# A hybrid decoder trunk: a third of the low weight halves made by accumulating transfers instead of GpSimd subtractions

## The chip, the cores and the metric

The kernel runs on one core of one Trainium2 chip. The metric is the device time of one execution in microseconds, given as the median of several runs. The engines are TensorE (PE for its matmuls, PEld for its weight loads), VectorE (DVE), ScalarE (ACT), GpSimd (POOL) and SyncE (SP, which issues most DMA transfers).

## The reference

Two pre-norm residual layers over 256 tokens of width 1024, all in float32. Each layer projects the normalised tokens by one matrix, feeds four token mixers with the parts, gates, projects and merges their outputs, and projects once more:

```
h = rms_norm(x, norm_g)
proj = einsum('bsd,de->bse', h, w_in)
u_lru, u_s5, qkv_ret, q_nsa, kv_nsa, bg_nsa, gate_paths, merge = split_columns(proj, IN_SIZES)
...                                    # four mixers: y_lru, y_s5, y_ret, y_nsa, each (256, 512)
ys = stack([y_lru, y_s5, y_ret, y_nsa]) * silu(gate_paths)
branch = einsum('bsnw,nwd->bsnd', ys, w_branch)
merged = sum(sigmoid(merge) * branch, axis=n)
x = x + einsum('bsd,de->bse', merged, w_out)
```

A final RMSNorm closes the stack. The inputs of both layers amount to over 100 MB of weights, each used once per execution.

## The kernel before

The products with the large weight matrices are cut into 36 chunks per layer (`CHUNKS`, lines 42 to 51), each a block of up to 512 output columns, and 34 of these into units (`UNITS`) of two 128-row slabs of 512 columns: 128 x 1024 numbers, 512 KB. There are 108 units a layer. SP loads them in order into a ring of four buffers, `raw` (`load_unit`, line 412; the loop at line 581). Transfers are issued in order, and each waits until its buffer is free.

The first 48 units of a layer are multiplied as they are ("native", lines 1515 to 1524). The last 60, `SPLIT_UNITS`, are split: a weight w becomes a high half, w rounded to the type `fp32r`, and a low half, w minus the high half; the activations are split in the same way. Each product is then three matmuls (`split_product`, line 1477): high x high, high x low, low x high. A split unit takes 12 matmuls of 512 columns on TensorE (24 of 256 columns in the two `glu` chunks). In this text the split units of a layer are numbered 0 to 59. Units 0 to 3 belong to the GLU of the S5 mixer, 4 to 7 to the gate of the retention branch, 8 to 11 to the first branch projection, 12 to 19 to a merge gate, and so on; 56 to 59 are the last of the output projection.

A split unit goes through these steps:

- SP loads it into `raw`.
- ScalarE casts it into `w_hi` (`cast_units`, line 664; the activation is recorded at line 660) and counts `hi_done`.
- GpSimd subtracts `w_hi` from `raw` into `w_lo` (`split_lo`, lines 632 to 643) and counts `lo_done`. For units 56 to 59 VectorE does that and counts `vlo_done`.
- TensorE waits for the low half (`wait_low`, line 377), which implies the high one.
- SP may load into the same `raw` buffer again when the low half is done (line 603).

`w_hi` and `w_lo` are rings of five (`N_SPLIT`): ScalarE and GpSimd wait for TensorE to be done with the unit five places earlier. Every engine runs its instructions in the order in which they are written. On ScalarE the casts stand between the other activations of the mixers: the casts of units 0 to 4 ahead of the eight gate activations of the RG-LRU mixer, those of 5 to 7 behind them, 8 to 11 behind the split of the first gated mixer output (`hi_of_gated`), 12 to 15 behind a square root and a table load, and in the sparse attention at the end some between the exponentials of one group of heads and the next (`attention_exp`, `cast_room`). On TensorE the chunks stand between the small products of the mixers. The compressed attention scores pass through a chain of small operations on VectorE (lines 1340 to 1357) whose result TensorE transposes ahead of the attention scores of the first group of heads.

Of the kernel before, what the change touches and what calls it, by code (L numbers as in the profile page):

```python
# [16 lines left out]
P = 128  # L17
# [3 lines left out]
DEPTH = 2  # L21
# [40 lines left out]
NU = len(UNITS)  # L62
for _u in range(NU):
    UNIT_USED.append((UNIT_USED[-1] if _u else 0) + (_u + 1 != UNIT_END[UNITS[_u][0]]))
N_RAW = 4
# [1 line left out]


NATIVE = ("u_s5", "cmp", "u_lru", "ret_v", "nsa_kv", "gate_s5", "gate_lru", "merge_s5_0", "merge_s5_1", "ret_q", "ret_k", "nsa_q")
SPLIT_UNITS = [u for u in range(NU) if CHUNKS[UNITS[u][0]][0] not in NATIVE]  # L70


LO_ON_VECTOR = ("out_0b", "out_1b")
VECTOR_UNITS = [u for u in SPLIT_UNITS if CHUNKS[UNITS[u][0]][0] in LO_ON_VECTOR]


def slot(s, l):
# [9 lines left out]
def vector_splits(upto):  # L87

    return sum(u < upto for u in VECTOR_UNITS)

V_NORM, V_CONV, V_CONVB, V_BA, V_BX, V_LAM, V_D, V_BGLU, V_LR, V_LI, V_DT, V_ROWS = (
# [7 lines left out]
    "cw1_loaded": 128, "cw_done": 1, "cw_loaded": 32, "diag_done": 2, "dt_exp": 1, "dt_rows": 1, "evacuated0": 16,  # L102
    "evacuated1": 16, "gate_tanh": 2, "h_done": 8, "hfull_done": 8, "hhi_done": 4, "hi_done": 60, "hidT_done": 2,
    "hid_arg": 1, "hid_ready": 1, "hid_tanh": 1, "hid_tm_ready": 2, "hlo_done": 8, "kcT_done": 1, "kcT_ready": 1,
    "kc_ready": 1, "lam_abs": 1, "lam_exp": 1, "lo_done": 56, "lru_act": 16, "lru_m2": 1, "lru_mm": 1,
    "lru_sqrt": 1, "mT_done": 2, "mag_arg": 1, "mag_exp": 1, "mhi_done": 2, "mlo_done": 2, "mt_free": 6,
    "nT_done": 2, "nT_ready": 2, "noT_done": 1, "no_cmp": 1, "nrope_ready": 2, "out_token": 2, "qkT_done": 2,
    "qkT_ready": 2, "raw_loaded0": 448, "raw_loaded1": 448, "raw_loaded2": 448, "raw_loaded3": 448, "rnT_done": 1,
    "rn_ready": 1, "ro_done": 4, "rope_ready": 2, "rrstd": 1, "rs_done": 4, "rs_ready": 4, "rstd": 2, "rvar": 1,
    "s5_split": 2, "sq": 4, "th_ready": 1, "th_sin": 3, "trig_done": 24, "unit_used": 73, "var": 2, "vbd_ready": 1,  # L110
    "vecT": 2, "vec_ready": 1, "vectors_loaded": 208, "vlo_done": 4, "wl_loaded": 64, "xT_done": 4, "x_half": 3,
    "xc_ready": 1, "y_done": 8, "y_used": 4, "yg_hi": 4, "yg_lo": 4, "yg_ready": 4, "yr_ready": 1, "z_arg": 1,
    "z_hi": 1, "z_lo": 1, "z_ready": 1, "z_tanh": 1}

TWO_PI = 2.0 * math.pi
PI2_A = 6.28125
# [57 lines left out]
def hybrid_trunk(nc, a, out):  # L174
# [4 lines left out]
    with ctx:  # L179
# [125 lines left out]
        raw_loaded = [sem(f"raw_loaded{i}") for i in range(N_RAW)]  # L305
        hi_done, lo_done, vlo_done, unit_used = sem("hi_done"), sem("lo_done"), sem("vlo_done"), sem("unit_used")
        chunk_done = sem("chunk_done")
        evacuated = [sem("evacuated0"), sem("evacuated1")]
        dve_order = sem("dve_order")
        xT_done = sem("xT_done")  # L310
# [66 lines left out]
        def wait_low(eng, u):  # L377


            if u in VECTOR_UNITS:  # L380
                eng.wait_ge(vlo_done, vector_splits(u + 1))
            else:
                eng.wait_ge(lo_done, splits(u + 1) - vector_splits(u + 1))

        def pr(name):

# [22 lines left out]
            return ap.to_broadcast(shape)  # L409


        def load_unit(sp, u, l, signal):

            c, k, n, w = UNITS[u]
            name = CHUNKS[c][0]
            dst = raw[:, u % N_RAW, 0:n * w].rearrange("p (k n) -> p k n", k=n)

            def load(d, src):
                sp.dma_start(d, src.rearrange("(k p) n -> p k n", p=P)).then_inc(signal, 16)

            def w_in(col, width, d=None):
                load(dst if d is None else d, a["w_in"][l][k * P:(k + n) * P, col:col + width])

            kind = name.split("_")[0]
            half = 512 * int(name[4] if kind == "out" else name[-1]) if kind in ("merge", "branch", "out") else 0
            if kind == "u":
                w_in(COL_S5 if name == "u_s5" else COL_LRU, w)
            elif kind == "ret":
                w_in(COL_RET + BW * "qkv".index(name[-1]), w)
            elif name == "nsa_q":  # L430
                w_in(COL_NQ, w)
            elif name == "nsa_kv":
# [107 lines left out]
        with nc.Block() as block:  # L540
            for l in range(DEPTH):
                @block.sync
                def _(queue):
# [37 lines left out]
                    for u in range(N_RAW, NU):  # L581
# [14 lines left out]
                        if u == UNIT_END[CHUNK["merge_nsa_0"]]:  # L596
# [2 lines left out]
                                load_vectors(queue, l + 1, VECTORS_A + VECTORS_B)  # L599
                            else:  # L600
                                queue.dma_start(g_row, a["final_norm_g"].unsqueeze(0).to_broadcast([P, D])).then_inc(g_loaded, 16)
                        if u - N_RAW in SPLIT_UNITS:
                            wait_low(sp, u - N_RAW)
                        else:
                            wait_unit_read(sp, u - N_RAW)
# [10 lines left out]
                def _(pool):  # L616
# [13 lines left out]
                    def split_lo(upto):  # L630

                        for s in range(done[0], splits(upto)):
                            u = SPLIT_UNITS[s]
                            c, _, n, w = UNITS[u]
                            if u in VECTOR_UNITS:
                                continue
                            gp.wait_ge(hi_done, s + 1)
                            if s >= N_SPLIT:
                                wait_unit_read(gp, SPLIT_UNITS[s - N_SPLIT])
                            elif l:  # L640
                                Layer(pool, l - 1).wait_ge(x_half, 3)
# [13 lines left out]
                def _(scalar):  # L655
# [8 lines left out]
                    def cast_units(upto):  # L664

                        for s in range(done[0], splits(upto)):
# [5 lines left out]
                            elif l:  # L672
                                Layer(scalar, l - 1).wait_ge(x_half, 3)
                            run(w_hi[:, slot(s, l), 0:n * w], raw[:, u % N_RAW, 0:n * w], ACT.Copy, hi_done)
                        done[0] = max(done[0], splits(upto))

                    def next_cast(name):
# [792 lines left out]
                def _(tensor):  # L1470
# [12 lines left out]
                    def chunk(name, part=2):  # L1483
# [11 lines left out]
                        for n in todo:  # L1495
                            u = u0 + n
                            _, k0, nk, _ = UNITS[u]
                            if name in NATIVE:
                                pe.wait_ge(raw_loaded[u % N_RAW], raw_target[u])
                            else:  # L1500
                                wait_low(pe, u)
# [1 line left out]
                            for kk in range(nk):  # L1503
# [8 lines left out]
                                def ht(lo, hi, pair=(h_hi, h_lo)):  # L1512
                                    return tuple(t[:, k, lo:hi] for t in pair)

                                if name in NATIVE:
                                    rw = raw[:, u % N_RAW, kk * w:(kk + 1) * w]
                                    if name in ("u_s5", "u_lru", "gate_s5", "gate_lru"):
                                        for m in range(4):
# [2 lines left out]
                                    else:  # L1521
                                        for t in range(TT):
                                            last = mm(ps[:, 512 * t:512 * t + w], h_full[:, k, t * P:(t + 1) * P], rw,  # L1523
                                                      start=st_, stop=sp_, skip_group_check=True)
                                elif kind == "u":
                                    for m in range(4):
                                        last = split_product(ps[:, m * T:(m + 1) * T], wt(m * P, (m + 1) * P), ht(0, T), st_ and m % 2 == 0, sp_)
                                elif kind == "glu":
# [361 lines left out]
```

## Time and profile before

| | |
|---|---|
| median of 3 runs | 858.96 us (858.77 to 859.5) |
| the profiled execution's own time | 857.93 us |
| its span in the trace | 856.1 us |
| PE busy | 825.7 us (96%) |
| DVE busy | 561.5 us (66%) |
| ACT busy | 312.2 us (36%) |
| POOL busy | 294.9 us (34%) |
| DMA, mean | 148 GB/s, 126.56 MB |

The two layers follow each other, and the second half of each has the split units: in the trace these lie at about 205 to 430 us and 626 to 850 us. GpSimd has next to nothing to do outside these stretches. A busy share tells little by itself here: what counts is whether a half is ready when TensorE comes to it. A timeline row gives the start and the length of an instruction, or of several alike that follow each other without a pause (then with their count behind the x).

### The profile page before, as it was taken

What the parts mean: (1) busy time and instruction counts of PE and PEld (TensorE: products, weight loads), DVE (VectorE), ACT (ScalarE), POOL (GpSimd) and SP (SyncE); (2) the same over time, 40 slices, a digit from 0 to 9 for tenths busy, and PEclk for the clock granted to TensorE, in tenths of its full rate; (3) what the DMA queues carried; (4) which work ended last, traced back from release to release, by engine and by line L of the source; (5) the groups of instructions that cost most, each with busy time, mean ns of one, the idle gap of its engine ahead of it and who ended that gap; (6) DMA issues with size and microseconds to landing.
All of it is one profiled execution on the core that took longest, in us unless ns stands there. A gap on an engine that the chain in (4) does not pass through costs nothing.

```text
span 856.1 us, 10220 instructions
## 1 busy us (share of the span) xinstructions
PE 825.7 (96%) x3918; PEld 611.4 (71%) x3918; DVE 561.5 (66%) x939; ACT 312.2 (36%) x519; POOL 294.9 (34%) x130
## 2 busy tenths in 40 slices
PE   8999999999899799999999999999998989999996
PEld 8864774446778688888888558644486867888885
DVE  2978999483697652634657889993828974435335
ACT  4411211015743545454425112110173534554542
POOL 1000000005567576767000000000157676665760
PEclk9999999999999899999999999999999998999999
DMA  8575544445245444444535745444554344445541
GB/s 250 140 245 144 192 127 122 130 141 201 94 127 168 123 148 148 120 152 152 153 70 161 244 119 198 143 125 127 146 172 147 116 132 129 137 130 170 172 147 50
DMA packets 86992, 126.56 MB, mean 148 GB/s; under 512 B 22072, under 2 KB 32672, under 8 KB 86944
## 3 DMA queue, kind: packets, MB, share of 16 engines
q1 hardware_dynamic: 86768, 125.88, 48.4%
q8 instruction: 31, 0.51, 0.2%
q14 instruction: 17, 0.14, 0.0%
q10 hardware_dynamic: 176, 0.04, 0.0%
HBM read 124.85 MB, written 1.05 MB: 147 GB/s over the span
## 4 chain that ended last, share of the span: by engine, by line
PE 59%; issue 29%; POOL 5%; DVE 3%; DMA 1%; ACT 1%; ACTq 0%; SPq 0%; POOLq 0%; DVEq 0%
PE proj L1480 29%; PE proj L1523 12%; PE proj L1519 6%; POOL w_lo L642 5%; PE M L1475 3%; PE M L1783 1%; PE M L1788 1%; DVE sc L1357 1%; PE M L1480 1%; DMA mt<-in_nsa_cv_w 1%; PE M L1753 1%; PE M L1807 1%; PE M L1806 1%; PE M L1624 1%; PE M L1805 1%
## 5 line engine op out<-in xcount | busy, mean ns | idle before, releaser
L642 POOL TENSOR_TENSOR w_lo<-raw,w_hi 128x1024 fp32r<-128x1024 f32 x112 | 286.3, 2586 | 504.9 <-ACT w_hi L660 473.9
L1523 PE MATMUL proj<-raw,h_full 128*128 128x512 f32 (+1 forms) x512 | 213.2, 572 | 0.0
L1523 PEld LDWEIGHTS proj<-raw,h_full 128*128 128x128 f32 x512 | 95.5, 190 | 104.7 <-issue 100.7
L660 ACT ACTIVATE w_hi<-raw 128x1024 fp32r<-128x1024 f32 x120 | 122.6, 1050 | 65.8 <-PE proj L1480 27.3
L1480 PE MATMUL proj<-w_hi,h_hi 128*128 128x512 f32 x320 | 128.4, 401 | 0.9 <-POOL w_lo L642 0.9
L1480 PE MATMUL proj<-w_lo,h_hi 128*128 128x512 f32 x320 | 124.9, 390 | 0.0
L1480 PE MATMUL proj<-w_hi,h_lo 128*128 128x512 f32 x320 | 124.8, 390 | 0.0
L1519 PE MATMUL proj<-h_full,raw 128*128 128x256 f32 x512 | 113.8, 381 | 0.0
L1519 PEld LDWEIGHTS proj<-h_full,raw 128*128 128x128 f32 x512 | 96.2, 190 | 14.1 <-issue 0.8
L1480 PEld LDWEIGHTS proj<-w_hi,h_hi 128*128 128x128 f32 x320 | 60.1, 188 | 14.4 <-issue 1.7
L1480 PEld LDWEIGHTS proj<-w_hi,h_lo 128*128 128x128 f32 x320 | 60.1, 188 | 13.0
L1480 PEld LDWEIGHTS proj<-w_lo,h_hi 128*128 128x128 f32 x320 | 60.2, 188 | 12.0 <-issue 0.5
L1480 PE MATMUL proj<-w_hi,ys_hi 128*128 128x512 f32 x128 | 52.9, 413 | 5.2 <-POOL w_lo L642 5.1
L1480 PE MATMUL proj<-w_lo,ys_hi 128*128 128x512 f32 x128 | 52.0, 406 | 0.0
L1480 PE MATMUL proj<-w_hi,ys_lo 128*128 128x512 f32 x128 | 51.9, 405 | 0.0
L660 ACT ACTIVATE sc<-sc,st 128x256 f32<-128x256 f32 x64 | 28.2, 442 | 57.2 <-DVE st L1373 57.2
L1123 DVE SCALAR_TENSOR_TENSOR mt<-mt,proj 128x1024 f32<-128x1024 f32 x12 | 14.7, 1222 | 39.6 <-PE proj L1480 39.6
L660 ACT ACTIVATE mt<-proj 128x1024 f32<-128x1024 f32 x16 | 16.3, 1019 | 63.1 <-PE proj L1523 54.4
L660 ACT ACTIVATE sc<-sc 128x512 f32<-128x512 f32 (+2 forms) x38 | 23.5, 665 | 42.0 <-DVE sc L1214 37.4
L1480 PEld LDWEIGHTS proj<-w_hi,ys_hi 128*128 128x128 f32 x128 | 25.4, 198 | 12.0 <-issue 5.9
L1480 PEld LDWEIGHTS proj<-w_hi,ys_lo 128*128 128x128 f32 x128 | 25.2, 197 | 5.6
L1480 PEld LDWEIGHTS proj<-w_lo,ys_hi 128*128 128x128 f32 x128 | 25.2, 197 | 5.2
(293 smaller groups left out, 1208.6 us busy)
## 6 DMA issues: line engine op xcount, KB each, us to landing
raw<-in_w_in SPq DMA_DIRECT2D x152, 512.0 KB, 3.5
raw<-in_w_branch SPq DMA_DIRECT2D x32, 512.0 KB, 3.8
raw<-in_w_out SPq DMA_DIRECT2D x16, 512.0 KB, 3.7
raw<-in_s_w_glu SPq DMA_DIRECT2D x8, 512.0 KB, 3.7
raw<-in_w_in SPq DMA_DIRECT2D x8, 256.0 KB, 2.6
merged<-in_nsa_ck_w SPq DMA_DIRECT2D x4, 512.0 KB, 5.3
mt<-in_nsa_ck_w SPq DMA_DIRECT2D x4, 512.0 KB, 6.9
merged<-in_nsa_cv_w SPq DMA_DIRECT2D x4, 512.0 KB, 5.8
```

Source lines behind the costliest of these rows:

```text
L642: nc.gpsimd.tensor_tensor(w_lo[:, slot(s, l), 0:n * w], raw[:, u % N_RAW, 0:n * w], w_hi[:, slot(s, l), 0:n * w].bitcast(f32), ALU.subtrac ...
L660: i = nc.scalar.activation(out_, in_, func, **kw)
L1123: v.scalar_tensor_tensor(m, m, 1.0, src, ALU.add, ALU.mult).then_inc(evac(full), 1)
L1357: i = v.tensor_tensor(cp[:, e_], cmp_s[:, e_], bc(coef[:, e_].unsqueeze(3), shape), ALU.mult)
L1475: return nc.tensor.transpose(dst, src, ident[0:rows_, 0:rows_])
L1480: last = mm(dst, left[i], right[j], start=start and n == 0, stop=stop and n == 2, skip_group_check=True)
L1519: last = mm(ps[:, m * T:(m + 1) * T], rw[:, m * P:(m + 1) * P], h_full[:, k, :], start=st_ and m % 2 == 0, stop=sp_, skip_group_check=True)
L1523: last = mm(ps[:, 512 * t:512 * t + w], h_full[:, k, t * P:(t + 1) * P], rw, start=st_, stop=sp_, skip_group_check=True)
L1624: last = mm(dst, cT[:, f, q, r], s5_h[:, p % 2, f, j, :], start=f == 0, stop=f == 1)
L1753: last = mm(M[:, e, at:at + 16], nqT[r, h, t * P:(t + 1) * P], kcT[r, (h // 2) * 16:(h // 2) * 16 + 16], start=True, stop=True)
L1783: last_ = mm(M[:, 2, at:at + P], nqT[r, 2 * h + n, 0:P], nkT[r, i, 0:P], start=True, stop=True)
L1788: mm(M[:, e, n * T:(n + 1) * T], nqT[r, 2 * h + n, P:T], nkT[r, i, :], start=True, stop=True)
```

## The change

Of the 56 split units whose low half GpSimd makes, every third (1, 4, 7, ..., 55; 19 a layer) gets it in another way. ScalarE, right after its cast, also writes the negated high half into `w_lo` (an activation Copy with scale -1, counted by `neg_done`). GpSimd waits for that and issues a DMA transfer that reads the unit's weights a second time from HBM and adds them onto `w_lo` (`accum_op=ALU.add`). TensorE waits for the landing of that transfer, on a semaphore of the `w_lo` buffer (`lo_added`). SP may refill the `raw` buffer of such a unit when the cast is done. `load_unit` takes the destination and the accumulate option as new arguments. The tests that told native chunks by name now ask whether the unit is split; the same units as before are native.

```diff
+ADDED_UNITS = [u for n, u in enumerate(v for v in SPLIT_UNITS if v not in VECTOR_UNITS) if n % 3 == 1]
...
+def added_splits(upto):
+
+    return sum(u < upto for u in ADDED_UNITS)
+
+
+def added_count(u, l):
+
+    here = slot(splits(u), l)
+    return sum((m, w) <= (l, u) and slot(splits(w), m) == here for m in range(DEPTH) for w in ADDED_UNITS)
...
             if u in VECTOR_UNITS:
                 eng.wait_ge(vlo_done, vector_splits(u + 1))
+            elif u in ADDED_UNITS:
+                eng.engine.wait_ge(lo_added[slot(splits(u), eng.l)], 16 * added_count(u, eng.l))
             else:
-                eng.wait_ge(lo_done, splits(u + 1) - vector_splits(u + 1))
+                eng.wait_ge(lo_done, splits(u + 1) - vector_splits(u + 1) - added_splits(u + 1))
...
-        def load_unit(sp, u, l, signal):
+        def load_unit(sp, u, l, signal, into=None, **how):
...
-            dst = raw[:, u % N_RAW, 0:n * w].rearrange("p (k n) -> p k n", k=n)
+            dst = (raw[:, u % N_RAW, 0:n * w] if into is None else into).rearrange("p (k n) -> p k n", k=n)
 
             def load(d, src):
-                sp.dma_start(d, src.rearrange("(k p) n -> p k n", p=P)).then_inc(signal, 16)
+                sp.dma_start(d, src.rearrange("(k p) n -> p k n", p=P), **how).then_inc(signal, 16)
...
-                        if u - N_RAW in SPLIT_UNITS:
+                        if u - N_RAW in ADDED_UNITS:
+                            sp.wait_ge(hi_done, splits(u - N_RAW + 1))
+                        elif u - N_RAW in SPLIT_UNITS:
                             wait_low(sp, u - N_RAW)
...
+                            if u in ADDED_UNITS:
+                                gp.wait_ge(neg_done, added_splits(u + 1))
+                                load_unit(pool, u, l, lo_added[slot(s, l)], w_lo[:, slot(s, l), 0:n * w], accum_op=ALU.add)
+                                continue
                             gp.wait_ge(hi_done, s + 1)
...
                             run(w_hi[:, slot(s, l), 0:n * w], raw[:, u % N_RAW, 0:n * w], ACT.Copy, hi_done)
+                            if u in ADDED_UNITS:
+                                act.wait_ge(hi_done, s + 1)
+                                run(w_lo[:, slot(s, l), 0:n * w], w_hi[:, slot(s, l), 0:n * w].bitcast(f32), ACT.Copy, neg_done, scale=-1.0)
```

On GpSimd, the first low halves of layer 0 stood in a row as follows (`w_lo<-raw,w_hi` is the subtraction; the first row has units 0 to 4):

```order
L642 TENSOR_TENSOR w_lo<-raw,w_hi 128x1024 [waits hi_done] x5
L642 TENSOR_TENSOR w_lo<-raw,w_hi 128x1024 [waits unit_used,hi_done]
L642 TENSOR_TENSOR w_lo<-raw,w_hi 128x1024 [waits chunk_done,hi_done]
L642 TENSOR_TENSOR w_lo<-raw,w_hi 128x1024 [waits unit_used,hi_done]
L642 TENSOR_TENSOR w_lo<-raw,w_hi 128x1024 [waits chunk_done,hi_done]
```

With the change GpSimd's row for units 0 to 8 is this (line numbers are those of the changed file):

```order
L671 TENSOR_TENSOR w_lo<-raw,w_hi 128x1024 [waits hi_done]
L442 DMA w_lo<-in_s5_w_glu 128x2x512 [waits neg_done]
L671 TENSOR_TENSOR w_lo<-raw,w_hi 128x1024 [waits hi_done] x2
L442 DMA w_lo<-in_w_in 128x2x512 [waits neg_done]
L671 TENSOR_TENSOR w_lo<-raw,w_hi 128x1024 [waits unit_used,hi_done]
L671 TENSOR_TENSOR w_lo<-raw,w_hi 128x1024 [waits chunk_done,hi_done]
L442 DMA w_lo<-in_w_in 128x2x512 [waits neg_done]
L671 TENSOR_TENSOR w_lo<-raw,w_hi 128x1024 [waits chunk_done,hi_done]
```

The transfer of a unit stands where its subtraction stood, and waits for ScalarE's negation instead of its cast.

On ScalarE, units 3 to 5 stood as follows around the gate activations of the RG-LRU mixer (`sc<-M,small` and `sc<-sc,small`):

```order
L660 ACTIVATE w_hi<-raw 128x1024 [waits raw_loaded3]
L660 ACTIVATE u_s<-proj 128x1024 [waits chunk_done]
L660 ACTIVATE w_hi<-raw 128x1024 [waits raw_loaded0]
L660 ACTIVATE sc<-M,small 128x256 [waits lru_mm]
L660 ACTIVATE sc<-M,small 128x256 x7
L847 ACT_TABLE_LOAD
L660 ACTIVATE sc<-sc,small 128x256 [waits lru_act]
L660 ACTIVATE sc<-sc,small 128x256 x7
L660 ACTIVATE w_hi<-raw 128x1024 [waits unit_used,raw_loaded1]
```

With the change the same place on ScalarE reads:

```order
L689 ACTIVATE w_hi<-raw 128x1024 [waits raw_loaded3]
L689 ACTIVATE u_s<-proj 128x1024 [waits chunk_done]
L689 ACTIVATE w_hi<-raw 128x1024 [waits raw_loaded0]
L689 ACTIVATE w_lo<-w_hi 128x1024 [waits hi_done]
L689 ACTIVATE sc<-M,small 128x256 [waits lru_mm]
L689 ACTIVATE sc<-M,small 128x256 x7
L879 ACT_TABLE_LOAD
L689 ACTIVATE sc<-sc,small 128x256 [waits lru_act]
L689 ACTIVATE sc<-sc,small 128x256 x7
L689 ACTIVATE w_hi<-raw 128x1024 [waits unit_used,raw_loaded1]
```

The negation of unit 4 now stands ahead of the gate activations, and the cast of unit 5 still behind them. TensorE's row is the same as before.

## Rows read from the trace of the kernel before

**Rows 1.** The page's busy us, shares and instructions of each engine.
```profile
PE 825.7 (96%) x3918; PEld 611.4 (71%) x3918; DVE 561.5 (66%) x939; ACT 312.2 (36%) x519; POOL 294.9 (34%) x130
```

**Rows 2.** Waits of PE: who for whom, us in total, times, longest us.
```profile
PE M L1475 <- DVE sc L1357: 9.1, 2, 4.5
PE proj L1480 <- POOL w_lo L642: 6.0, 4, 2.6
```

**Rows 3.** The page's costliest groups: busy us, mean ns, idle before and releaser.
```profile
L642 POOL TENSOR_TENSOR w_lo<-raw,w_hi 128x1024 fp32r<-128x1024 f32 x112 | 286.3, 2586 | 504.9 <-ACT w_hi L660 473.9
L660 ACT ACTIVATE w_hi<-raw 128x1024 fp32r<-128x1024 f32 x120 | 122.6, 1050 | 65.8 <-PE proj L1480 27.3
```

**Rows 4.** Timeline, 282 to 287.5 us: start, us, engine, line, operation, [idle before].
```profile
282.15 4.73 DVE L1357 TENSOR_TENSOR sc<-sc,st 128x128 f32<-128x128 f32 x2
...
284.34 2.39 POOL L642 TENSOR_TENSOR w_lo<-raw,w_hi 128x1024 fp32r<-128x1024 f32 x1
...
286.94 0.67 PE L1475 MATMUL M<-const,sc 128*128 128x128 f32 x2 [4.54 <-DVE sc L1357]
```

**Rows 5.** Windows: us, busy (x) PE, PEld, DVE, ACT, POOL; PEclk, DMA share, GB/s.
```profile
235.80:239.20 3.40, 3.40 (x10) 2.63 (x9) 3.40 (x2) 0.02 (x1) 3.40 (x2) 0.50 0.77 217
287.00:293.80 6.80, 6.80 (x24) 5.57 (x25) 2.25 (x3) 1.33 (x2) 4.39 (x2) 0.50 0.76 223
```

**Rows 6.** Timeline of PE: the first product of unit 8.
```profile
234.74 0.47 PE L1480 MATMUL proj<-w_hi,ys_hi 128*128 128x512 f32 x1 [2.56 <-POOL w_lo L642]
```

**Rows 7.** DMA issues: count, KB each, median us from issue to landing.
```profile
raw<-in_w_branch SPq DMA_DIRECT2D x32, 512.0 KB, 3.8
...
mt<-in_nsa_ck_w SPq DMA_DIRECT2D x4, 512.0 KB, 6.9
```

**Rows 8.** The chain that ended last: start us, us, what.
```profile
430.59 0.55 POOL st L522
```

**Rows 9.** Timeline of ACT: casts of units 4, then 8 to 11.
```profile
208.15 1.05 ACT L660 ACTIVATE w_hi<-raw 128x1024 fp32r<-128x1024 f32 x1
209.09 3.02 ACT L660 ACTIVATE sc<-M,small 128x256 f32<-128x256 f32 x8
...
231.03 3.88 ACT L660 ACTIVATE w_hi<-raw 128x1024 fp32r<-128x1024 f32 x4
```

**Rows 10.** Timelines of DVE, POOL and PE around unit 7.
```profile
227.19 1.58 DVE L1272 SCALAR_TENSOR_TENSOR sc<-sc 128x1024 f32<-128x1024 f32 x1 [1.77 <-ACT sc L660]
...
224.30 3.38 POOL L642 TENSOR_TENSOR w_lo<-raw,w_hi 128x1024 fp32r<-128x1024 f32 x1
...
227.98 0.39 PE L1480 MATMUL proj<-w_hi,h_hi 128*128 128x512 f32 x1
```

**Rows 11.** Timelines of POOL and PE: subtraction and first product of unit 13.
```profile
252.31 2.77 POOL L642 TENSOR_TENSOR w_lo<-raw,w_hi 128x1024 fp32r<-128x1024 f32 x1
...
255.32 0.39 PE L1480 MATMUL proj<-w_hi,h_hi 128*128 128x512 f32 x1
```

**Rows 12.** Timeline of ACT: casts of units 25, 31, 37 and 43.
```profile
298.75 1.04 ACT L660 ACTIVATE w_hi<-raw 128x1024 fp32r<-128x1024 f32 x1
...
322.53 1.04 ACT L660 ACTIVATE w_hi<-raw 128x1024 fp32r<-128x1024 f32 x1
...
345.18 1.04 ACT L660 ACTIVATE w_hi<-raw 128x1024 fp32r<-128x1024 f32 x1
...
369.06 1.04 ACT L660 ACTIVATE w_hi<-raw 128x1024 fp32r<-128x1024 f32 x1
```

**Rows 13.** The chain: units 24 and 25, 30 and 31, 36 and 37, 42 and 43.
```profile
305.05 5.48 PE proj L1480 x24
...
327.67 5.51 PE proj L1480 x24
...
350.31 5.51 PE proj L1480 x24
...
372.96 5.51 PE proj L1480 x24
```

More of the change, by code:

```diff
@@ L69, with by_name @@
 NATIVE = ("u_s5", "cmp", "u_lru", "ret_v", "nsa_kv", "gate_s5", "gate_lru", "merge_s5_0", "merge_s5_1", "ret_q", "ret_k", "nsa_q")
-SPLIT_UNITS = [u for u in range(NU) if CHUNKS[UNITS[u][0]][0] not in NATIVE]
+def by_name(u):
+    return CHUNKS[UNITS[u][0]][0]
+SPLIT_UNITS = [u for u in range(NU) if by_name(u) not in NATIVE]
 LO_ON_VECTOR = ("out_0b", "out_1b")
-VECTOR_UNITS = [u for u in SPLIT_UNITS if CHUNKS[UNITS[u][0]][0] in LO_ON_VECTOR]
+VECTOR_UNITS = [u for u in SPLIT_UNITS if by_name(u) in LO_ON_VECTOR]
+ADDED_UNITS = [u for n, u in enumerate(v for v in SPLIT_UNITS if v not in VECTOR_UNITS) if n % 3 == 1]
 def slot(s, l):
@@ L104 @@
     "hid_arg": 1, "hid_ready": 1, "hid_tanh": 1, "hid_tm_ready": 2, "hlo_done": 8, "kcT_done": 1, "kcT_ready": 1,
-    "kc_ready": 1, "lam_abs": 1, "lam_exp": 1, "lo_done": 56, "lru_act": 16, "lru_m2": 1, "lru_mm": 1,
+    "kc_ready": 1, "lam_abs": 1, "lam_exp": 1, "lo_done": 37, "lru_act": 16, "lru_m2": 1, "lru_mm": 1,
     "lru_sqrt": 1, "mT_done": 2, "mag_arg": 1, "mag_exp": 1, "mhi_done": 2, "mlo_done": 2, "mt_free": 6,
[L107 to L113, printed above, removed]
+    "nT_done": 2, "nT_ready": 2, "neg_done": 19, "noT_done": 1, "no_cmp": 1, "nrope_ready": 2, "out_token": 2,
+    "qkT_done": 2, "qkT_ready": 2, "raw_loaded0": 448, "raw_loaded1": 448, "raw_loaded2": 448, "raw_loaded3": 448,
+    "rnT_done": 1, "rn_ready": 1, "ro_done": 4, "rope_ready": 2, "rrstd": 1, "rs_done": 4, "rs_ready": 4,
+    "rstd": 2, "rvar": 1, "s5_split": 2, "sq": 4, "th_ready": 1, "th_sin": 3, "trig_done": 24, "unit_used": 73,
+    "var": 2, "vbd_ready": 1, "vecT": 2, "vec_ready": 1, "vectors_loaded": 208, "vlo_done": 4, "wl_loaded": 64,
+    "xT_done": 4, "x_half": 3, "xc_ready": 1, "y_done": 8, "y_used": 4, "yg_hi": 4, "yg_lo": 4, "yg_ready": 4,
+    "yr_ready": 1, "z_arg": 1, "z_hi": 1, "z_lo": 1, "z_ready": 1, "z_tanh": 1}
 TWO_PI = 2.0 * math.pi
@@ L307, in hybrid_trunk @@
         chunk_done = sem("chunk_done")
+        neg_done = sem("neg_done")
+        lo_added = [sem(f"lo_added{i}") for i in range(N_SPLIT)]
         evacuated = [sem("evacuated0"), sem("evacuated1")]
@@ L1497, in chunk @@
                             _, k0, nk, _ = UNITS[u]
-                            if name in NATIVE:
+                            if u not in SPLIT_UNITS:
                                 pe.wait_ge(raw_loaded[u % N_RAW], raw_target[u])
@@ L1513, in ht @@
                                     return tuple(t[:, k, lo:hi] for t in pair)
-                                if name in NATIVE:
+                                if u not in SPLIT_UNITS:
                                     rw = raw[:, u % N_RAW, kk * w:(kk + 1) * w]
@@ L1524, in chunk @@
                                                       start=st_, stop=sp_, skip_group_check=True)
-                                elif kind == "u":
+                                elif name in ("u_s5", "u_lru", "gate_s5", "gate_lru"):
                                     for m in range(4):
```

## The prediction

> **What bounds the kernel now.** I read the busy shares first, then TensorE's waits, then the margins in the second half of a layer (the only part that is changed), and last the durations from which the new step is priced. TensorE is busy 825.7 of 856.1 us [rows 1], so there are some 30 us to win in all. Of its waits the trace names two that reach the weights' low halves: 9.1 us in 2 waits for VectorE's line 1357, one in each layer, and 6.0 us in 4 waits for GpSimd's subtraction [rows 2]. GpSimd is therefore no bound over the span; it matters where TensorE stands right behind it. I number the 60 split units of a layer 0 to 59, in the order of use; the change takes 1, 4, 7 and so on up to 55 (19 of them). All times below are of layer 0; layer 1 repeats the pattern 420.6 us later, as the two equal waits of rows 2 say.
>
> **What is removed.** 38 subtractions of 2.59 us each on GpSimd [rows 3], 98 us of its work, and with each of them its hold on an input that VectorE shares: in the trace two VectorE operations on 128x128 elements, an elementwise product each, take 4.73 us together while GpSimd subtracts, and the subtraction of unit 22 fills exactly the second half of that stretch, 284.34 to 286.73 [rows 4]. TensorE stands still for 4.54 us for that result, to 286.94 [rows 4]. Without that subtraction the second product can start at 284.4 as the first ends: 2.3 us less wait in each layer. TensorE is granted half speed, the lower of 1.2 and 2.4 GHz, from 287.0 to 293.8 after that standstill, and from 235.8 to 239.2 after the shorter one of 2.56 us [rows 5, 6]. At half speed half of the time is lost: 3.4 us of the longer stretch, 1.7 us of the shorter. The shorter wait should bring the shorter slow stretch: 1.7 us more. The gain is 2.3 + 1.7 = 4.0 us a layer. The Trainium skill (SBUF — State Buffer, Who interferes with whom) says that a VectorE instruction with two SBUF inputs is shut out for the whole of a GpSimd instruction that reads SBUF; the trace agrees with it in the 4.73 us, and the new transfer's descriptors are no such instruction.
>
> **What is added.** ScalarE gets 38 negations of the size of its casts, 1.05 us each [rows 3], with a wait for its own cast ahead, about 0.05 us. Then GpSimd issues, and the transfer lands. Call D the time from the moment at which both the negation and GpSimd's work ahead are over to the landing. The trace of before has no DMA from GpSimd and none that adds, so D is bounded from its neighbours. Low: 3.5 us, no dearer than a plain 512 KB load (3.8 us at the median [rows 7]) with the issue free and a little luck. High: 9.5 us, if GpSimd is held as long as by a subtraction (2.6 [rows 3]) and the landing is as slow as that of the slower group of 512 KB loads, several in flight (6.9 [rows 7]). I take 0.6 for the issue (a tiny GpSimd operation takes 0.55 [rows 8]), 3.8 for a plain load, and half of that again, 1.9, because the destination must be read as well: D = 6.3, close to the 6.9 of rows 7. The raw loads go on beside it, on the same engines, and the weights of these units are read twice, 38 x 512 KB = 19.9 MB more.
>
> The Trainium skill (DMA: Bandwidth & Descriptors, Anatomy of one DMA — SWDGE (gpsimd) path) gives a transfer from GpSimd a fixed 2.0 us and its bytes at 436 GB/s; counted for both operands, 1.05 MB, that is an estimate of 4.4 us. No row of this trace shows such a transfer.
>
> **Place by place, for D = 6.3.** A unit is late if cast end + 1.1 (or the end of GpSimd's work ahead, if later) + D passes the moment TensorE wants it.
> - Unit 8, and 4 and 7 ahead of it. The negation of unit 4 stands between its cast at 208.15 and the gate activations at 209.09 [rows 9]. VectorE and then the cast of unit 8 at 231.03 hang on these, and TensorE waits for unit 8 until 234.74 [rows 6, 9]. So +1.1, less 0.4 because VectorE's line 1272 (1.58 us, behind unit 7's subtraction [rows 10]) gets free: 235.4. Unit 7 itself: GpSimd is free for it at 224.30 [rows 10] + 1.1 = 225.4, lands 231.7, wanted at 227.98 [rows 10] + 1.1; 2.6 late. From unit 7's start to unit 8's are 4.2 us of TensorE work (231.7 + 4.2 = 235.9): net +1.2.
> - Unit 13. GpSimd reaches it at 252.31, TensorE wants it at 255.32, and now it is ready just in time [rows 11]. Landing at 252.35 + 6.3 = 258.65: +3.3. A standstill of that size brought half speed before, so +1.7.
> - Units 31, 37 and 43 have casts at 322.53, 345.18 and 369.06 [rows 12]; each is the second half of a run of 24 products that starts at 327.67, 350.31 and 372.96 [rows 13], so wanted 2.6 later: 330.3, 352.9, 375.6. Cast end + 1.1 + 6.3 is 331.0, 353.6, 377.5: +0.7, +0.7, +1.9.
> - Unit 25: its cast ends at 299.8 and it is wanted 2.6 us into the run from 305.05, at 307.6 [rows 12, 13]; 299.8 + 7.4 = 307.2, so nothing, with 0.4 to spare. The same difference of cast end and use is 7 us or more for the other 12 (1, 10, 16, 19, 22, 28, 34, 40, 46, 49, 52, 55), and GpSimd has no queue ahead of them that uses it up: nothing. The 1.05 us of the negations there lie in ScalarE's gaps. If that cover were gone, each negation would cost its 1.1 us, as at unit 4. Nothing is queued on GpSimd behind a wait for a negation that TensorE needs at once: the next cast comes 1.05 us later, where a subtraction of 2.4 is saved.
> - SP gets the raw slot back at the cast instead of the subtraction, 1.3 us or more earlier. Raw data is not what TensorE waits for, so it gives nothing and only brings loads beside the new transfers.
>
> Sum: 1.2 + 3.3 + 1.7 + 0.7 + 0.7 + 1.9 - 4.0 = 5.5 us a layer, 11.0 in all. On the profiled execution's own 857.93 us that is 868.9; the median of the runs is 1.0 above that execution, so 869.9: **870 us**.
>
> **The rivals.**
> 1. *A short transfer, and the change is faster.* For D = 3.5: unit 8 +0.7, unit 13 +0.5 (255.85 against 255.32), the rest in time, gain 4.0: -2.8 a layer, -5.6 in all, 853 us. For D = 4.4: unit 13 +1.4, unit 8 +0.7, so -1.9 a layer: 855 us. For it: the plain load's 3.8 us at the median, and that only the landing of the last byte counts. Against it: the issue and the second operand would have to be nearly free. The skill's estimate of 4.4 us above falls here. Chance 0.28.
> 2. *No difference.* At D = 4.7 to 4.9 unit 13's 1.8 and its possible half speed, unit 8's 0.7 and unit 43's 0.3 meet the 4.0. 859 us. Chance 0.10.
> 3. *A slow transfer.* For D = 7.7: unit 8 +2.6, unit 13 +4.7 and 2.5 of half speed, unit 25 +1.0 (299.8 + 1.1 + 7.7 against 307.6), units 31, 37, 43 +2.1, +2.1, +3.3 with 3.4 of half speed, less 4.0: 17.7 a layer, 894 us. At D = 9.5 it passes 910. For it: two raw loads are set free just when unit 13's transfer is issued, and share the engines. Chance 0.15.
> 4. *The relief of VectorE does not come*, because writing the descriptors shuts VectorE out as the subtraction did: then the 4.0 a layer is not gained, 878 us. The trace can't exclude it: it shows only subtractions beside VectorE. Chance 0.05.
>
> The forecast itself has 0.42; its own range, D from 5.5 to 7, is 861 to 883.
>
> **How the numbers follow.** From about D = 4.7 on the change costs. The range goes from D = 3.5 to a little over 7.7: 852 to 896, leaving out the slowest part of rival 3. A measurement can tell about 0.2% (1.7 us) from nothing. Slower: forecast, rivals 3 and 4, 0.62. Same: 0.10. Faster: 0.28.
>
> **What will show it.** Right, if the page of the changed kernel has a transfer into w_lo from GpSimd with 5.5 to 7 us from issue to landing; if TensorE's waits have a new row that ends with that DMA, longest 2 to 4 us, at unit 13; if the wait for line 1357 falls from 9.1 to about 4.5 us; and if ScalarE has 38 more operations of 1.05 us. Wrong, if that landing takes under 4.7 us, or if the late units are others: then it is an engine's queue, and not the transfer, that decides. If the wait for line 1357 stays at 9.1, rival 4 holds.

## The result, and the profile after

The changed kernel takes 897.24 us at the median of four runs (895.58 to 898.63), against 858.87 us for the kernel before on the same chip: a ratio of 1.0449, with a 95% interval of 1.0426 to 1.0472. The profiled execution took 895.58 us, its span is 893.8 us and its mean granted TensorE clock 0.967, against 0.987 before. The forecast said slower, by 11 us; it is slower by 38 us, just above the range.

From the page of the changed kernel, against [rows 1, 3, 7]: the busy line, the two groups of GpSimd and the new one of ScalarE (busy us, mean ns | idle before, with what ended it), and two issue rows (KB each, median us from issue to landing). Line 671 is the subtraction (642 before), line 442 the new transfer, line 689 the activations of ScalarE (660 before), line 1512 the split products (1480 before), line 1389 the old 1357, and line 1157 the old 1125, the sum of the merge. (In the experiments' kernels the same lines stand one or two further down, or, where nothing is transferred, a few further up.)

```profile
PE 838.1 (94%) x3918; PEld 620.3 (69%) x3918; DVE 561.4 (63%) x939; ACT 351.5 (39%) x557; POOL 233.5 (26%) x130
...
L671 POOL TENSOR_TENSOR w_lo<-raw,w_hi 128x1024 fp32r<-128x1024 f32 x74 | 188.0, 2617 | 459.5 <-ACT w_hi L689 449.6
...
L442 POOL DMA_DIRECT2D w_lo<-in_w_in x24 | 29.0, 1206 | 98.9 <-ACT w_lo L689 98.4
...
L689 ACT ACTIVATE w_lo<-w_hi 128x1024 fp32r<-128x1024 f32 x38 | 40.3, 1060 | 1.2
...
w_lo<-in_w_in POOLq DMA_DIRECT2D x24, 512.0 KB, 6.9
...
w_lo<-in_w_branch POOLq DMA_DIRECT2D x8, 512.0 KB, 8.8
```

What was to be moved has moved: 38 subtractions are gone, 38 negations of 1.06 us are there, and 38 x 512 KB come a second time. GpSimd is less busy by 61 us and TensorE more busy by 12.4 us for the same 3918 products, which I read as time at the lower clock. The span grew by 37.7 us, so the other 25.3 us are standstills. Which ones, the waits of TensorE say (us in total, times, longest):

```profile
PE proj L1512 <- DMA w_lo<-in_w_in: 14.6, 9, 5.3
PE M L1507 <- DVE sc L1389: 11.5, 2, 5.7
PE proj L1512 <- DMA w_lo<-in_s_w_glu: 4.9, 2, 3.5
PE M L1507 <- DVE merged L1157: 4.7, 2, 2.4
PE proj L1512 <- DMA w_lo<-in_w_branch: 3.5, 2, 2.8
```

Against [rows 2]: the 6.0 us for GpSimd's subtractions are gone, 23.0 us in 13 waits for the new transfers have come, the wait behind VectorE's product has grown from 9.1 to 11.5 us where it was to be halved, and there is a new one at line 1157.

Laying the two timelines of TensorE side by side, unit by unit, gives what each place cost in both layers together, the slow clock behind it included (a unit's lateness against before, less that of the unit ahead):

| place | forecast, both layers | measured in the two traces |
|---|---|---|
| unit 1, with the wait for ScalarE behind it | 0 | +8.9 |
| units 7 to 9 | +2.4 | -0.5 (layer 0 -3.6, layer 1 +3.1) |
| unit 10 | 0 | +3.5 |
| units 12 and 13 | +10.0 | +9.8 (unit 12 -1.3, unit 13 +11.0) |
| VectorE's line 1389, ahead of unit 20 | -8.0 | +3.2 |
| units 31, 37, 43 | +6.6 | +3.2 |
| line 1157, ahead of unit 51 | 0 | +8.2 |
| elsewhere | 0 | +1.3 |
| sum | +11.0 | +37.6 |

The measured column compares one execution of each kernel, and a single place in it is good to a few us only. Layer 0 up to unit 13 is the same program in two of the kernels below (the one without unit 52's transfer, and the changed kernel with a wait), yet units 12 and 13 cost 5.8 and 8.9 us there, and here 2.3. Here the granted clock stayed at 1.00 behind the standstill of 2.63 us; without unit 52's transfer it was 0.50, half speed, behind one of 3.05 us.

In layer 1, 2.1 us of what stands under unit 1 are a wait for ScalarE: 2.88 us instead of 0.81 for the gate activations of the RG-LRU mixer, ahead of which unit 4's cast waited 0.97 us for its raw load and the negation took 1.06.

Three things stand behind the table. The first is how long the transfer takes. Of the 38, eleven land 5.6 to 5.9 us after the issue, six after 6.4 to 6.7, and the other 21 after 7.0 to 10.5. GpSimd and SP around the transfer of unit 13, then GpSimd around that of unit 31 (start us, us, what; in brackets the idle time before and what ended it):

```profile
252.86 1.20 POOL L442 DMA_DIRECT2D w_lo<-in_w_in  x1
253.64 5.16 POOL L671 TENSOR_TENSOR w_lo<-raw,w_hi 128x1024 fp32r<-128x1024 f32 x2
...
252.94 6.26 SPq L442 DMA_DIRECT2D raw<-in_w_in  x4
...
262.35 0.50 PE L1512 MATMUL proj<-w_hi,h_hi 128*128 128x512 f32 x1 [2.63 <-DMA w_lo<-in_w_in]
...
333.58 1.20 POOL L442 DMA_DIRECT2D w_lo<-in_w_in  x1 [9.37 <-ACT w_lo L689]
...
339.32 0.50 PE L1512 MATMUL proj<-w_hi,h_hi 128*128 128x512 f32 x1 [0.35 <-DMA w_lo<-in_w_in]
```

At unit 31 SP's next load goes out only 4 us later (the one before it went out 1.46 us ahead of the transfer): the first packet moves 1.9 us after the issue, and TensorE goes on 5.74 us after it. At unit 13 SP issues two raw loads 0.1 and 0.5 us after GpSimd: the first packet moves only after 4.9 us, and TensorE goes on after 9.49. From 1.0 to 4.5 us behind the issue only packets of the raw loads move. That is no chance meeting. SP issues in order. The subtraction of unit 12 sets unit 12's raw slot free, unit 13's has been free since its cast, and the end of that same subtraction is what lets GpSimd go on to its transfer. So wherever GpSimd has no gap between a subtraction and the next transfer, two raw loads start beside it.

The second is VectorE's product. VectorE and GpSimd at the place of [rows 4]:

```profile
289.31 5.92 DVE L1389 TENSOR_TENSOR sc<-sc,st 128x128 f32<-128x128 f32 x2
...
286.83 4.73 POOL L671 TENSOR_TENSOR w_lo<-raw,w_hi 128x1024 fp32r<-128x1024 f32 x2 [9.87 <-PE proj L1512]
291.49 1.22 POOL L442 DMA_DIRECT2D w_lo<-in_w_branch  x1
292.26 2.81 POOL L671 TENSOR_TENSOR w_lo<-raw,w_hi 128x1024 fp32r<-128x1024 f32 x1
...
295.29 0.69 PE L1507 MATMUL M<-const,sc 128*128 128x128 f32 x2 [5.74 <-DVE sc L1389]
```

The subtraction of unit 22 is gone, but that of unit 23 takes its place 0.77 us after the issue began, and takes 2.81 us instead of 2.39: so the two products take 5.92 us instead of 4.73, where 2.4 was forecast. The clock shows the price of the longer standstill (us, busy times, then the granted clock; before it was 6.8 us at half speed [rows 5], here 6.8 us, to 302.2, behind a stretch with almost no product in it):

```profile
292.00:295.40 3.40, 0.11 (x1) 0.11 (x2) 3.23 (x1) 0.00 (x0) 3.07 (x2) 0.55 0.82 225
295.40:298.80 3.40, 3.40 (x15) 2.88 (x15) 0.00 (x0) 1.33 (x2) 1.38 (x1) 0.50 1.07 224
```

The third was nowhere in the forecast: an elementwise sum of VectorE, 1024 wide, now coincides with a subtraction behind the transfer of unit 52.

```profile
411.52 3.72 DVE L1157 TENSOR_TENSOR merged<-merged,mt 128x1024 f32<-128x1024 f32 x1
...
408.20 1.20 POOL L442 DMA_DIRECT2D w_lo<-in_w_out  x1 [1.93 <-ACT w_lo L689]
408.97 5.18 POOL L671 TENSOR_TENSOR w_lo<-raw,w_hi 128x1024 fp32r<-128x1024 f32 x2
...
415.30 1.97 PE L1507 MATMUL M<-const,merged 128*128 128x128 f32 x8 [2.35 <-DVE merged L1157]
```

### The profile page after: what moved, and what is told of

Same layout as the page of the kernel before. It is cut to its first block, busy times and chain, and to the rows that moved or that the text cites. A ratio compares the mean times of both kernels' runs of the same rounds, so it can differ in the third digit from the quotient of the medians.

```text
span 893.8 us, 10222 instructions
## 1 busy us (share of the span) xinstructions
PE 838.1 (94%) x3918; PEld 620.3 (69%) x3918; DVE 561.4 (63%) x939; ACT 351.5 (39%) x557; POOL 233.5 (26%) x130
## 4 chain that ended last, share of the span: by engine, by line
PE 58%; issue 14%; POOL 9%; DMA 8%; DVE 8%; ACT 2%; SPq 0%; ACTq 0%; POOLq 0%; DVEq 0%
PE proj L1555 23%; PE proj L1512 15%; PE proj L1551 10%; POOL w_lo L671 7%; DMA w_lo<-in_w_in 6%; PE M L1507 2%; PE M L1512 2%; DVE sc L1389 1%; PE M L1656 1%; DMA raw<-in_s_w_glu 1%; PE M L557 1%; POOL w_lo L442 1%; ACT w_hi L689 1%; DMA mt<-in_nsa_cv_w 1%; PE M L1785 1%
## 5 line engine op out<-in xcount | busy, mean ns | idle before, releaser
L671 POOL TENSOR_TENSOR w_lo<-raw,w_hi 128x1024 fp32r<-128x1024 f32 x74 | 188.0, 2617 | 459.5 <-ACT w_hi L689 449.6
L1512 PE MATMUL proj<-w_hi,h_hi 128*128 128x512 f32 x320 | 131.6, 411 | 14.8 <-DMA w_lo<-in_w_in 14.6
L1512 PE MATMUL proj<-w_lo,h_hi 128*128 128x512 f32 x320 | 127.0, 397 | 0.0
L1512 PE MATMUL proj<-w_hi,h_lo 128*128 128x512 f32 x320 | 126.6, 395 | 0.0
L442 POOL DMA_DIRECT2D w_lo<-in_w_in x24 | 29.0, 1206 | 98.9 <-ACT w_lo L689 98.4
L689 ACT ACTIVATE w_lo<-w_hi 128x1024 fp32r<-128x1024 f32 x38 | 40.3, 1060 | 1.2
```

What stands on the lines that cost most here:

```text
L442: sp.dma_start(d, src.rearrange("(k p) n -> p k n", p=P), **how).then_inc(signal, 16)
L689: i = nc.scalar.activation(out_, in_, func, **kw)
L1512: last = mm(dst, left[i], right[j], start=start and n == 0, stop=stop and n == 2, skip_group_check=True)
```

## The experiments

Each ratio is against runs of the kernel before on the same chip, whose medians were 858.4, 858.5 and 857.0 us in the three groups. The lists of units are set by one line; where a variant transfers other units, the counts per layer follow it.

**Is it the adding?** The transfer without its addition, all else as changed.

```
-  load_unit(pool, u, l, lo_added[slot(s, l)], w_lo[:, slot(s, l), 0:n * w], accum_op=ALU.add)
+  load_unit(pool, u, l, lo_added[slot(s, l)], w_lo[:, slot(s, l), 0:n * w])
```

> The changed kernel with plain transfers instead of accumulating ones (the low halves are then the full weights, so the output is not the reference's). Theory Q (queueing: in the trace of the changed kernel a transfer that is issued together with two raw loads sends its first packet 4 to 5 us later and lands after 7.7 to 10 us, one alone after 5.6 to 5.9): the slow ones stay slow, median landing 6.5 us or more, 887 to 897 us. Theory A (the adding itself, a read and a write of the destination, makes the transfer long): landing falls to that of a raw load, 3.5 to 5 us, everywhere, and the time to 865 to 875 us.

877.07 us, 1.0219 [1.0198, 1.0240]. Issue row, and the two waits that answer to it:

```profile
w_lo<-in_w_in POOLq DMA_DIRECT2D x24, 512.0 KB, 5.1
```

```profile
PE M L1507 <- DVE sc L1389: 10.6, 2, 5.3
PE proj L1512 <- DMA w_lo<-in_w_in: 7.7, 4, 3.6
```

A plain transfer lands 4.3 to 5.2 us after its issue when alone, 4.7 in the middle (first packet after 1.6 us), and 5.0 to 7.5 beside two raw loads (after some 2.9), and its issue is a row of 0.74 us on GpSimd instead of 1.20. So the addition costs 1 us alone and about 3 us beside raw loads, and with it go 20 of the 38 us. The other half stays with a transfer that adds nothing: VectorE's wait and the queueing (the first packet that comes late beside raw loads) are there too. Neither theory has the whole.

**Is it the raw loads beside it?** SP holds the first of the two raw loads, and with it those behind it, until the transfer has landed.

```
+  if u - N_RAW + 1 in ADDED_UNITS:
+      wait_low(sp, u - N_RAW + 1)
```

> SP holds back the raw load that was issued at the same moment as each accumulating transfer, until that transfer has landed. Theory Q: every landing takes 5.5 to 6.6 us, TensorE's waits for w_lo transfers fall from 23 us to below 10, and the time to 872 to 886 us, unless raw data becomes late. Theory A and theory V (VectorE or the next subtraction holds back the writing of descriptors): landings stay at 7.7 to 10 us in the same places, time 893 us or more.

942.05 us, 1.0976 [1.0949, 1.1003]. Its issue row, then the wait for the transfers:

```profile
w_lo<-in_w_in POOLq DMA_DIRECT2D x24, 512.0 KB, 5.9
```

```profile
PE proj L1514 <- DMA w_lo<-in_w_in: 18.4, 12, 4.0
```

The landing falls from 6.9 to 5.9 and from 8.8 to 6.5 us at the median, over all 38 from 7.4 to 6.0 (5.7 to 8.1). The subtraction behind the issue still starts 0.78 us after it at most places, and the first packet moves after 1.9 us there: the raw loads beside the transfer delay it, not that subtraction. The time is not won, because SP issues in order: the held load holds those behind it, casts come late (ScalarE waits 73.6 us for raw loads of `in_w_in`, 1.0 us in the changed kernel), and with them the transfers. TensorE's waits for them add up to 37 us, where below 10 was expected, and the time is 56 us above the upper end of what was expected; holding loads back is no cure.

**One unit where the overlap is certain.** Only unit 13 is transferred.

```
-  ... if n % 3 == 1]
+  ... if n == 13]
```

> Only unit 13 of each layer comes by transfer. Two raw loads are set free with its issue. Theory Q (queueing behind them): it lands about 9 us after the issue, 6 us after TensorE wants it, with a slow-clock stretch behind: 8 to 10 us a layer, 874 to 880 us. If the landing were the 5.7 us of an undisturbed transfer: 3.3 us late, 5 us a layer, 868 to 870 us. The price of the prediction for this unit was 5.0 us a layer.

875.60 us, 1.0199 [1.0167, 1.0232]. Its waits:

```profile
PE proj L1513 <- DMA w_lo<-in_w_in: 12.8, 2, 7.1
PE M L1508 <- DVE sc L1390: 9.1, 2, 4.5
PE proj L1513 <- POOL w_lo L672: 6.0, 4, 2.6
```

The two transfers land 10.25 and 8.85 us after the issue, with two raw loads issued 0.1 and 0.5 us behind each. TensorE waits 7.1 and 5.7 us for them and has half speed for a while after; everything else is as before. That is 9 us a layer for one unit, where the forecast's sum had 5.0. In the changed kernel unit 13 costs 11.0 us in both layers together: in the first TensorE comes to it 4 us late already, where GpSimd is only 0.6 us late, and stands 2.6 us without a slow clock behind it; in the second it stands 5.3 us, with half speed behind.

**Only the units with much time to spare**, 16, 19, 22, 28, 34, 40, 46, 49, 52 and 55.

```
-  ... if n % 3 == 1]
+  ... if n in (16, 19, 22, 28, 34, 40, 46, 49, 52, 55)]
```

> Only 10 units a layer come by transfer, those whose cast ended 7.5 us or more before use (16, 19, 22, 28, 34, 40, 46, 49, 52, 55). If only late landings at 1, 7, 10, 13, 31, 37, 43 cost: no TensorE wait on a transfer, 858 to 866 us, the rest being VectorE waits of changed phase. If each transfer or negation costs for itself, 10 of 19: about 879 us.

884.16 us, 1.0299 [1.0271, 1.0328]: far from expected. Waits, then GpSimd around the issue of unit 16:

```profile
PE M L1508 <- DVE sc L1390: 11.4, 2, 5.7
PE proj L1513 <- DMA w_lo<-in_w_in: 9.8, 2, 4.9
```

```profile
260.72 3.36 POOL L672 TENSOR_TENSOR w_lo<-raw,w_hi 128x1024 fp32r<-128x1024 f32 x1
264.02 1.34 POOL L443 DMA_DIRECT2D w_lo<-in_w_in  x1
...
266.59 5.13 POOL L672 TENSOR_TENSOR w_lo<-raw,w_hi 128x1024 fp32r<-128x1024 f32 x2
```

Unit 16 is cast at 259.56, but GpSimd still has subtractions to do and issues at 264.02; the transfer lands 9.25 us later, and TensorE stands 4.90 us, until 273.41. The time from cast to use was not to spare: with units 7, 10 and 13 subtracted again, GpSimd's queue used it up. The waits for VectorE are those of the changed kernel.

**The late units only**, from 25 on (11 a layer).

```
-  ... if n % 3 == 1]
+  ... if n % 3 == 1 and n >= 25]
```

> Only units 25 to 55 (11 a layer) by transfer, none in the first part. From the trace of the changed kernel: units 31, 37 and 43 some 1.5 us a layer together, unit 51 about 4 us: 867 to 872 us. It would be 880 us or more if transfers cost in proportion to their number (11 of 19 of the loss).

870.92 us, 1.0154 [1.0124, 1.0184]. Its waits:

```profile
PE M L1508 <- DVE merged L1158: 4.8, 2, 2.4
PE proj L1513 <- DMA w_lo<-in_w_in: 3.5, 6, 0.8
```

As expected: some 14 us, of which the late units' own waits are 3.5 us, in six waits (31, 37 and 43 of each layer), and the sum of line 1157 (1158 here) 4.8. With what the clock adds the two places cost 5.4 and 5.1 us. That leaves some 24 us of the loss for units 1 to 22.

**VectorE and what stands behind the issue.** First unit 22 alone, then 22 and 23, so that no subtraction follows the issue at once.

```
-  ... if n % 3 == 1]
+  ... if n == 22]            # the other kernel: n in (22, 23)
```

> Only unit 22 of each layer comes by transfer; all else as before. Theory P (the prediction: without the subtraction of unit 22 VectorE's second product starts as the first ends): the TensorE wait for line 1389 (1357 before) falls from 9.1 to about 4.5 us, 850 to 853 us. Theory S (as the trace of the changed kernel suggests, the issue and the subtraction of unit 23 behind it shut VectorE out in its place): the wait is 9 to 12 us, 859 to 865 us. The trace tells what VectorE's second product waits out.

> Units 22 and 23 of each layer come by transfer, so no subtraction stands behind unit 22 on GpSimd until unit 24. Theory S (a subtraction behind the issue shuts VectorE out): the wait for line 1389 falls to about 4.5 us, 850 to 855 us. Theory V (the issue itself, the writing of descriptors, shuts VectorE out): the second product ends with the first issue, 1.2 us later than under S, or with the second; the wait is 6 to 8 us or more.

Unit 22 alone: 861.63 us, 1.0041 [1.0028, 1.0054]. VectorE and GpSimd:

```profile
281.82 6.07 DVE L1390 TENSOR_TENSOR sc<-sc,st 128x128 f32<-128x128 f32 x2
...
284.00 1.35 POOL L443 DMA_DIRECT2D w_lo<-in_w_branch  x1
284.94 2.80 POOL L672 TENSOR_TENSOR w_lo<-raw,w_hi 128x1024 fp32r<-128x1024 f32 x1
```

Units 22 and 23: 854.21 us, 0.9957 [0.9944, 0.9970], faster than before. The same view, then TensorE's waits:

```profile
281.82 2.60 DVE L1390 TENSOR_TENSOR sc<-sc,st 128x128 f32<-128x128 f32 x2
...
284.00 2.59 POOL L443 DMA_DIRECT2D w_lo<-in_w_branch  x2
286.48 2.54 POOL L672 TENSOR_TENSOR w_lo<-raw,w_hi 128x1024 fp32r<-128x1024 f32 x1
...
PE M L1508 <- DVE sc L1390: 4.8, 2, 2.4
PE proj L1513 <- DMA w_lo<-in_w_branch: 4.5, 4, 1.3
```

The issue of a transfer does not shut VectorE out: the first product ends with the subtraction ahead, at 284.1, and the second runs while the two transfers are issued, so that both are done at 284.42. One more subtraction 0.94 us behind the issue does, for its whole length. So the relief is real and can be had, but not by taking unit 22 alone. By place it brings 5.3 and 4.9 us in the two layers, slow clock included (the forecast had 4.0), and 2.8 us of it in each go to the two transfers, of which the second lands 13.0 us after its issue.

**ScalarE's share.** The negations stay, every unit is subtracted, no transfer is issued.

```
-  load_unit(pool, u, l, lo_added[slot(s, l)], w_lo[...], accum_op=ALU.add)
-  continue
```

> The negations stay on ScalarE, in w_lo, but GpSimd subtracts all 56 low halves as before and there are no added transfers. If ScalarE's 38 x 1.06 us matter only at unit 4 (and so unit 8): +1.1 us a layer, perhaps a changed phase beside it, 859 to 864 us. If ScalarE's work is what costs: 880 us or more.

864.29 us, 1.0073 [1.0046, 1.0100]: about 6 us, somewhat more than expected. Its waits:

```profile
PE M L1501 <- ACT sc L683: 3.7, 2, 1.9
...
PE M L1501 <- DVE u_s L1277: 2.5, 2, 2.1
```

The forecast charged one negation of 1.1 us a layer. ScalarE's work is late at several places by about a negation each. VectorE's sum of line 1157 (1151 here) is waited for 0.9 us in each layer already, with no transfer in the kernel.

**Line 1157.** The changed kernel without the transfer of unit 52.

```
-  ... if n % 3 == 1]
+  ... if n % 3 == 1 and n != 52]
```

> The changed kernel without the transfer of unit 52. In its trace VectorE's line 1157 is shut out by the subtraction behind that issue, and TensorE loses 2.35 us and a slow-clock stretch at unit 51, about 4 us a layer. If that subtraction's changed start is the cause: the wait goes, 8 us less, 887 to 890 us. If it is chance of the whole schedule: unchanged, 895 us or more.

891.02 us, 1.0380 [1.0351, 1.0408]: 6.2 us less than the changed kernel by the medians, 5.9 by the ratios, a little short of expected. The wait for line 1157 is gone from TensorE's waits. In the changed kernel the transfer of unit 52 lands in time; what it costs is that the next subtraction meets VectorE's sum.

**GpSimd made to wait for VectorE's chain.** One wait ahead of unit 20's subtraction, so that nothing of GpSimd runs beside lines 1340 to 1357: in the kernel before (first), and in the changed one (second).

```
+  if s == 20:
+      gp.wait_ge(cp_ready, 1)
```

> The kernel before, with no transfer on GpSimd; GpSimd waits for the end of VectorE's chain up to line 1357 before it subtracts unit 20, whose low half was ready 9.3 us before use. If the three subtractions of units 20 to 22 are what lengthens that chain from about 2 to 6.7 us, TensorE's 4.5 us wait goes, and the slow-clock stretch of 6.8 us behind it, up to 8 us a layer: 843 to 850 us. If VectorE was slow for itself: no change or slower.

> The changed kernel with the wait of b1_cp on GpSimd ahead of unit 20. If the loss at line 1389 is the same mechanism in both kernels (subtractions of 20, 21 and 23 shut VectorE out): the wait of 11.5 us and the slow clock behind it go, 16 to 20 us less than the changed kernel, 877 to 882 us. If the issue or its landing lengthens that chain: 890 us or more.

Before plus the wait: 842.84 us, 0.9826 [0.9811, 0.9840]. VectorE and GpSimd:

```profile
280.42 0.18 DVE L1356 TENSOR_TENSOR st<-st,bgate 128x16 f32<-128x16 f32 x1
280.63 0.49 DVE L1359 TENSOR_TENSOR sc<-sc,st 128x128 f32<-128x128 f32 x2
...
281.20 11.79 POOL L644 TENSOR_TENSOR w_lo<-raw,w_hi 128x1024 fp32r<-128x1024 f32 x5 [7.30 <-DVE sc L1359]
```

The two products take 0.49 us instead of 4.73, TensorE no longer waits there, and the mean clock rises from 0.987 to 0.994. By the rows of before that should give 4.54 us of standstill and half of the 6.8 us at half speed [rows 4, 5] in each layer, 15.9 in all; by the medians it is 15.6. It is the relief that the changed kernel was to bring in part, had whole.

The changed kernel plus the wait: 888.38 us, 1.0364 [1.0324, 1.0403], only 7 us (by the ratios) to 9 us (by the medians) less than without, where 16 to 20 were expected. Its waits:

```profile
PE proj L1514 <- DMA w_lo<-in_w_in: 21.7, 10, 6.5
PE proj L1514 <- DMA w_lo<-in_w_branch: 8.7, 3, 4.2
```

The wait for VectorE is gone, but unit 22's transfer is now issued at 297.72 and lands 8.8 us later, and TensorE stands 4.19 us for it. With subtractions GpSimd catches up; with a transfer of 9 us it does not.

**The best version:** the kernel before with that wait, and the cast of unit 8 one step earlier.

```
+  cast_units(UNIT_END[CHUNK["branch_s5_0"]] - 1)    # ahead of hi_of_gated("s5")
```

> As b1_cp, and ScalarE casts unit 8 ahead of the split of the gated output instead of behind it, so that GpSimd can subtract it up to 3 us earlier. If TensorE's wait of 2.56 us at unit 8 is for that subtraction alone: 4 us a layer less than b1_cp. But the subtraction then lies beside VectorE's products for the gated output and may hold them back by up to 2.4 us: then 0 to 2 us a layer, or none.

841.63 us, 0.9811 [0.9793, 0.9830]. The waits for GpSimd's subtractions are gone (5.5 us with the first edit alone), but TensorE waits 4.4 us for VectorE's line 1254 (2.5 with the first edit alone) and 2.4 for line 1113 (none): the second edit brings about 1 us, which the intervals do not tell from nothing.

## Why the prediction was wrong

The sign was right, and for part of the reason: the transfer is slower than the subtraction, and units with no time to spare wait for it. The size was wrong by 27 us, and one step of the sum had the wrong sign.

- **The relief of VectorE** ("Without that subtraction the second product can start at 284.4") failed: -8.0 forecast, +3.2 measured, 11 us of the 27. I took one subtraction out of the row and did not ask what moves up into its place. The subtraction of unit 23 does, 0.77 us behind the issue. It is rival 4's outcome and not its mechanism: descriptors shut nobody out (units 22 and 23 together, 2.60 us), the next subtraction does (unit 22 alone, 6.07 us). The Trainium skill's rule (SBUF — State Buffer, Who interferes with whom) is that a VectorE instruction with two SBUF inputs is shut out while a GpSimd instruction reads SBUF. These rows agree with it, 2.60 us against 6.07; it was the order behind the issue that I left out.
- **D = 6.3** was right for a transfer alone and wrong for the rest. At unit 31 it is 6.1 us from the negation's end to the landing (333.19 to 339.27), and units 31 and 37 cost 0.6 and 0.5 us in layer 0 against 0.7 and 0.7. Beside two raw loads it is 7.7 to 10.5 us. Rival 3 had this mechanism ("two raw loads are set free just when unit 13's transfer is issued"), with a chance of 0.15; but the forecast's sum used one D for all places, and let the loads beside it cost nothing. Since the two loads are set free by the very subtraction that GpSimd finishes before it issues, it was to be read from the code. It gives most of unit 1 (+8.9, less the 2.1 us of ScalarE) and unit 10 (+3.5), some 10 us of the 27. Both had been called in time by a misreading: the forecast's own rule asks for 1.1 + 6.3 = 7.4 us from the cast's end to the use, and unit 1 has 7.1 in the trace of before (201.35 to 208.43); unit 10 has 9.7, but GpSimd is busy with unit 9 until 236.98, and 0.4 us are left to the use at 243.64. The median of the issue row, 6.9 us, lies within the 5.5 to 7 that I had named as proof, and hides two groups of landings; the second row's 8.8, and late units that I had not named, were the sign.
- **Unit 13** came out near the forecast by luck. Its place cost 9.8 us against 10.0, but of the terms 3.3 + 1.7 a layer none holds: in layer 0 TensorE stood 2.6 us with no slow clock behind, in layer 1 5.3 us with 2.6 more from the clock, and at unit 12, ahead of it, 1.3 us were won, mostly since the waits of 0.47 and 0.44 us for that unit's subtraction fell away. The landing took 9.4 and 8.5 us instead of 6.3, and TensorE came later than before. Alone, the unit costs 9 us a layer.
- **Line 1157** (+8.2) was missed. Taking out the transfer of unit 52 brings back 6 us, and TensorE's wait there is gone: so most of it is a matter of when the next subtraction starts. I had looked for VectorE's relief at one place and nowhere for its opposite.
- **The negations** were charged only at unit 4. On their own they cost about 6 us, 0.9 us of wait a layer at line 1157 among them.
- **Units 7 to 9** came to -0.5 us against +2.4. In layer 0 TensorE was late already, so that unit 8's standstill and its slow clock fell away (-3.6); in layer 1 unit 7's transfer landed 8.8 us after its issue and was waited for 4.96 us.
- **Units 31, 37 and 43** cost 3.2 us in all against 6.6: the first two as forecast, and unit 43 less, since its cast came 1.3 us earlier against TensorE than before.

The parts measured alone don't add up to 38 us and are not meant to: each delay gives the next unit time. How the 38 us divide among the places is known only as well as the single executions above agree. What stays open: why the transfer that was issued first gets its first packet last. The runs show that it does so with raw loads beside it and not without, adding or not; where in the machine it waits, they don't show.

## What to carry to other kernels

Before a transfer is priced, ask which event lets it start and what else that same event sets free: a price from transfers that run alone holds only where nothing else starts with it. When an instruction is taken away because it shuts another engine out, look at the instruction behind it; unless that is gone too, the lock only moves. Where one engine's bulk work meets another's short chain that TensorE waits for, one wait that keeps them apart (16 us here) was worth more than making the bulk work cheaper.

## What the runs showed of the hardware

- A 512 KB transfer issued by GpSimd with nothing else starting beside it landed 4.7 us after its issue when plain (4.3 to 5.2) and 5.6 to 5.9 us when adding into SBUF; each of the 16 DMA engines was busy about 2.1 us with the first and 3.4 us with the second. The Trainium skill's estimate used in the prediction (DMA: Bandwidth & Descriptors, Anatomy of one DMA — SWDGE (gpsimd) path), 4.4 us for adding, is 1.2 us or more too low here.
- The row of such an issue on GpSimd is 1.20 us long when adding and 0.74 when plain, where SP's loads go out 0.4 us apart. Behind an adding one (units 13 and 22) the next subtraction's row starts 0.77 us after the issue's; at unit 22 it is 2.8 us long, and 2.35 behind the plain one.
- With two loads from SP issued 0.1 and 0.5 us after it, the first packet of the adding transfer moved after 4.9 us at unit 13 (3.5 to 5.2 at all such places of the changed kernel) instead of 1.9.
- VectorE's elementwise product of 128x128 elements took 0.28 us with GpSimd idle or issuing a transfer, 2.4 beside one subtraction, and up to 3.75 where a subtraction followed the issue.
